# The first gate's row multiplied into the out projection's weights instead of into its result

## The reference

```
sh1, sc1, gt1, sh2, sc2, gt2 = split(silu(c) @ w_ada + b_ada)
h = rms_norm(x) * (1 + sc1) + sh1
proj = h @ w_in                      # split into HGRN2, attention, gates ga, gb
merged = sigmoid(ga) * (y_a @ w_branch_a) + sigmoid(gb) * (y_b @ w_branch_b)
x = x + (1 + gt1) * (merged @ w_out)
h2 = rms_norm(x) * (1 + sc2) + sh2
u_gate, u_val = split(h2 @ w_up)
x = x + (1 + gt2) * ((gelu(conv(u_gate)) * u_val) @ w_down)
return rms_norm(x)
```

## Time and profile before

| what | us |
| --- | --- |
| median of three runs | 940.07 |
| profiled execution, its own time | 939.99 |
| span of the profiled execution | 938.1 |
| TensorE busy with matmuls | 909.8 |
| GpSimd busy | 442.5 |
| VectorE busy | 441.2 |
| ScalarE busy | 363.7 |

### The profile page before, as it was taken

The page is one execution under the profiler, slowest core; times in us unless marked ns, Lnnn a source line. Parts: engine busy times, 40 slices in busy tenths (PEclk is TensorE's granted clock), DMA queues, the critical chain, the costliest instruction groups (busy, mean ns, idle before and its releaser), DMA issues.

```text
span 938.1 us, 11737 instructions
## 1 busy us (share of the span) xinstructions
PE 909.8 (97%) x4468; PEld 768.6 (82%) x4468; DVE 441.2 (47%) x712; ACT 363.7 (39%) x482; POOL 442.5 (47%) x390
## 2 busy tenths in 40 slices
PE   2999999999999999999999999999999999999996
PEld 1888898988878888888888888888888888888885
DVE  4743468684548978976624526222232222200005
ACT  5433335252443323353422237544444444421113
POOL 2589335253424432454554645554444554444554
PEclk9999999999999999999999999999999999999998
DMA  9842221212352858244526221422233222232212
GB/s 312 276 133 90 90 90 45 90 45 91 106 164 90 270 185 264 90 152 168 198 90 224 89 90 46 134 89 89 93 115 105 89 89 89 93 132 90 89 45 90
DMA packets 94087, 115.52 MB, mean 123 GB/s; under 512 B 2206, under 2 KB 84314, under 8 KB 94046
## 3 DMA queue, kind: packets, MB, share of 16 engines
q1 hardware_dynamic: 94046, 114.95, 37.1%
HBM read 112.81 MB, written 2.13 MB: 123 GB/s over the span
## 4 chain that ended last, share of the span: by engine, by line
PE 46%; issue 29%; POOL 20%; DVE 3%; ACT 1%; DMA 1%; POOLq 0%; SPq 0%; DVEq 0%; ACTq 0%
PE bank L1070 45%; POOL w_lo L679 19%; DMA x_in<-in_x_dram 1%; DVE bank L1530 0%; DVE bank L2032 0%; DVE x L2033 0%; PE bank L1073 0%; DVE xn_ffn L1924 0%; POOL masks L616 0%; ACT w_hi L758 0%; POOL masks L653 0%; DVE h_tmp2a L1586 0%; ACT h_tmp L785 0%; POOLq L709 0%; POOL xg L733 0%
## 5 line engine op out<-in xcount | busy, mean ns | idle before, releaser
L679 POOL TENSOR_TENSOR w_lo<-w_raw,w_hi 128x512 fp32r<-128x512 f32 x292 | 390.5, 1368 | 442.4 <-ACT w_hi L758 437.5
L1070 PE MATMUL bank<-h_hi,w_hi 128*128 128x512 f32 (+1 forms) x880 | 340.8, 390 | 0.1
L1070 PE MATMUL bank<-h_lo,w_hi 128*128 128x512 f32 (+1 forms) x880 | 337.2, 386 | 0.0
L1070 PE MATMUL bank<-h_hi,w_lo 128*128 128x512 f32 (+1 forms) x880 | 261.8, 386 | 0.0
L758 ACT ACTIVATE w_hi<-w_raw 128x2048 fp32r<-128x2048 f32 x72 | 137.6, 1911 | 223.4 <-PE bank L1070 223.4
L1070 PEld LDWEIGHTS bank<-h_hi,w_lo 128*128 128x128 f32 x880 | 165.9, 188 | 33.3
L1070 PEld LDWEIGHTS bank<-h_lo,w_hi 128*128 128x128 f32 x880 | 165.9, 188 | 32.9
L1070 PEld LDWEIGHTS bank<-h_hi,w_hi 128*128 128x128 f32 x880 | 165.4, 189 | 33.1 <-POOL h_lo L666 0.3
L1070 PE MATMUL bank<-w_hi,act_hi 128*128 128x512 f32 x176 | 68.5, 389 | 0.0
L1070 PE MATMUL bank<-w_lo,act_hi 128*128 128x512 f32 x176 | 68.5, 389 | 0.0
L1070 PE MATMUL bank<-w_hi,act_lo 128*128 128x512 f32 x176 | 68.5, 389 | 0.0
(11 more groups left out here) (254 smaller groups left out, 1115.2 us busy)
## 6 DMA issues: line engine op xcount, KB each, us to landing
w_raw<-in_w_in_dram SPq DMA_DIRECT2D x32, 1024.0 KB, 5.2
w_raw<-in_w_up_dram SPq DMA_DIRECT2D x22, 1024.0 KB, 5.1
ada<-in_w_ada_dram SPq DMA_DIRECT2D x16, 1024.0 KB, 5.3
w_raw<-in_w_down_dram SPq DMA_DIRECT2D x11, 1024.0 KB, 4.8
ada<-in_w_ada_dram SPq DMA_DIRECT2D x16, 512.0 KB, 8.7
w_raw<-in_w_out_dram SPq DMA_DIRECT2D x4, 1024.0 KB, 5.0
x_in<-in_x_dram SPq DMA_DIRECT2D x4, 512.0 KB, 5.0
w_raw<-in_w_in_dram SPq DMA_DIRECT2D x8, 256.0 KB, 7.4
```

The lines of the kernel that those rows point to most:

```text
L679: ins = pool.tensor_tensor(wlo[slot][:, cols], raw[slot][:, cols], whi[slot][:, cols].bitcast(F32), ALU.subtract)
L1070: return pe.matmul(o, lhsT, rhs, start=start, stop=stop, **kw)
```

## The change

A new function, `gate_out(u)`, multiplies the whole raw unit (128x2048) in place by the matching 512 numbers of the gate's row, repeated for the four blocks of rows, on VectorE. ScalarE's high part of an out unit waits for it by a new semaphore. The multiplication of the result banks is gone, and `added` now waits for the bank itself.

```diff
+        gated_out = sem("gated_out")
...
                     if u == 3:
                         act.wait_ge(hi_done, 3)
+                if U_OUT <= u < U_UP:
+                    act.wait_ge(gated_out, u - U_OUT + 1)
                 high_part(u % 2, 16 * (u // 2 + 1))
...
+            def gate_out(u):
+
+                c = (u - U_OUT) // 2
+                if u == U_OUT:
+                    dve.wait_ge(gate_in[0], 16)
+                dve.wait_ge(raw_in[u % 2], 16 * (u // 2))
+                rows = raw[u % 2][:, :].rearrange("p (k c) -> p k c", c=512)
+                gate = g1_row[:, 512 * c:512 * c + 512].unsqueeze(1).broadcast_to([P, KT // 2, 512])
+                tt(rows, rows, gate, ALU.mult).then_inc(gated_out, 1)
+
             def residual(c, t):
 
-                gated(c, t)
                 added(c, t)
 
-            def gated(c, t):
-
-                b = ready(dve, ("out", c, t))
-                link(tt(b[:, :], b[:, :], g1_row[:, 512 * c:512 * c + 512], ALU.mult))
-
             def added(c, t):
 
-                b, cols = bank[BANKS["out", c, t][0]], slice(512 * c, 512 * c + 512)
+                b, cols = ready(dve, ("out", c, t)), slice(512 * c, 512 * c + 512)
                 release(tt(x1[:, t, cols], x1[:, t, cols], b[:, :], ALU.add), ("out", c, t))
...
                 xn_again(1, slice(0, D))
-                gated(1, 2)
                 make_h2(0, 0)
...
+                if U_OUT <= u < U_UP - 2:
+                    gate_out(u + 2)
                 evacuate(u)
+                if U_OUT - 2 <= u < U_OUT:
+                    gate_out(u + 2)
```

## The result

The changed kernel took 943.39 us (median of 8 runs, 942.71 to 944.09), the kernel before on the same chip 940.19 us (8 runs, 939.28 to 940.49). The ratio is 1.0035, with a 95% interval of 1.0026 to 1.0044: slower by 3.2 us. The forecast was 943.3.

The account below looks back on a forecast made before the run. TensorE, busy 97% of the span, was taken as the bound, already waiting 0.23 us for unit 39's low part. Terms +3.1, +0.5 and -0.3 gave +3.3 on 939.99, hence 943.3 us; 8-in-10 range 941.2 to 945.5.

Parts of the forecast that it names:

- The multiplication costs 2.28: On VectorE, each new 128x2048 multiplication of a raw weight unit by the gate's repeated row takes 2.28 us.
- Unit 38: high part +2.34, TensorE waits 0.7 to 2.3: ScalarE's high part of unit 38 starts 2.34 us later, so TensorE waits 0.7 to 2.3 us for GpSimd's low part.
- Unit 39: +3.1, and +0.5 by collisions: Unit 39 starts 3.1 us later through its multiplication, plus 0.5 from VectorE colliding with GpSimd in unit 37's evacuation.
- +3.7 by the exclusion of VectorE and GpSimd: If unit 40's multiplication held off GpSimd's first instruction of unit 39 by 0.3 or more, the sum became +3.7, not +3.3.
- A wait of 1.2 to 2.9 at unit 39: TensorE finishes unit 38 by 534.7 at most, then waits 1.2 to 2.9 us for unit 39's low part from GpSimd.
- Rival 2: TensorE's pace falls to matmuls 0.43 us apart after a new wait: 945.3, or 947 if at both; chance 0.10.
- matmuls 0.43 apart behind the waits: Sign that the prediction is wrong: TensorE's matmuls after the new waits start 0.43 us apart, against 0.227.
- Units 40 and 41 have cover: Their later weights delay nothing: no TensorE wait at either unit, with 1.4 us of cover at unit 41, plus 0.7 more.
- -0.3 at the second transposition: Tile 3's dropped right-column multiplication shortens TensorE's 0.58 us wait before the second transposition by 0.3, bounds 0 and 0.6.
- The sum: Over the whole kernel, +3.1 for unit 39's multiplication, +0.5 for collisions and -0.3 at the second transposition: +3.3 us.

Follow-up runs that it names:

- early38: The change, with unit 38's multiplication moved ahead of unit 36's evacuation so that only unit 39's chain is late: 945.44 us, ratio 1.0057.
- right_clear: The change for the right columns only (units 40 and 41), whose multiplications also wait until GpSimd finishes the unit before: 944.06 us, ratio 1.0036.
- left: The change for the left columns only (units 38 and 39); right columns multiplied in the result as in the kernel before: 943.85 us, ratio 1.0037.
- final: The change, with unit 38's multiplication ahead of unit 36's evacuation, unit 39's within unit 37's, and ScalarE's high parts of both units earlier: 939.03 us, ratio 0.9993.
- only38: The change, but unit 39's weights are not multiplied and its high part does not wait for the gate: 942.82 us, ratio 1.0027.
- extra1024: The kernel before, plus one unused GpSimd instruction on 1024 columns ahead of unit 38's low part: 943.39 us, ratio 1.0029.

## Why the prediction was right, and where not

The time was right, and the start of unit 39 (536.06, forecast 535.8 to 536.8). By steps:

- *The multiplication costs 2.28.* Three of the four took 2.28 to 2.29 (512.53, and the pair of 4.49 from 526.55, whose records overlap a little), and the fourth 3.10 where GpSimd worked beside it. The repeated row of the gate costs nothing more.
- *Unit 38: high part +2.34, TensorE waits 0.7 to 2.3.* High part at 514.90, +2.19; GpSimd at 516.90, 6.47 long, wait 1.98. Right, at the upper end, as GpSimd lost 1.4 to collisions. The upper bound does not follow from the rows it names: 517.0 and the 5.94 of the earlier trace rows give 522.97 and a wait of 1.6, not 523.7 and 2.3. The 0.7 on top came without a row, and the run used 0.4 of it.
- *Unit 39: +3.1, and +0.5 by collisions.* The high part moved by 3.32 (525.60 to 528.92). The four VectorE instructions that collided lost 0.4, 1.1, 0.4 and 1.1, nearly the series of the prediction, 2.9 in all against 2.6 before. The evacuation ended 0.2 later (526.63; 0.3 by the marks), not 0.5. The mis-sized term is the collisions, by 0.2 to 0.3.
- *+3.7 by the exclusion of VectorE and GpSimd.* The second multiplication of the pair ended at 531.04, 0.13 after GpSimd had started at 530.91, and GpSimd took its undisturbed 5.03. Nothing was lost here.
- *A wait of 1.2 to 2.9 at unit 39.* This is the step that failed in the profiled execution. The prediction said that unit 38 would end by 534.7 and TensorE would wait for the rest. No wait stood there: TensorE worked at half clock in unit 38 and ended it at 536.06. (By their mean clocks, several of the other executions may have kept the pace and waited as forecast.) Rival 2, the fall of the pace, happened, and was given 1 in 10. Its price of 2.0 was near (1.8), but it was added to the sum (945.3), when at the first wait it lies beside the time that unit 39's low part takes anyway. One of the prediction's own marks of error, matmuls 0.43 apart behind the waits, was seen, and it belonged to a cost that was covered. early38 shows the case in which it isn't: +5.0, the bare sum of a late unit 39 and a slow stretch, less the gain at the second transposition. That the time came out within 0.1 of the forecast in spite of this step is owed to the cover, which the prediction had not seen; so in part it is luck.
- *Why I gave it 1 in 10.* The nearest row was a wait of 1.30 with full pace behind it. In these runs the pace was kept behind 0.80, 1.09 and 1.30, and lost behind 1.98, 1.99, 2.35, 2.82 and 3.25. The forecast of 0.7 to 2.3 reached well into the second group, so 1 in 10 was too little. The Trainium skill (TensorE: Matmul & The Clock Gate, section "What's actually happening") names just the two clocks that were seen.
- *Units 40 and 41 have cover.* Yes, no wait there, although unit 40's low part took 7.08. The cover at unit 41 was 1.6 before and not 1.4, because TensorE came at 554.56 and not at 554.4. right_clear shows how small it is: 4.5 us later cost 3.0.
- *-0.3 at the second transposition.* The wait went from 0.58 to 0.21, a gain of 0.37; by the marks the second transposition came 3.13 later where unit 40 had come 3.44 later, a gain of 0.31. left takes the right half out and has 0.6 again.
- *The sum.* By the marks unit 39 starts 3.51 later (3.39 in the times of the profiles, as unit 36 itself started 0.12 earlier), the second transposition 3.13, and the end 3.22; the medians differ by 3.2. What took back the last 0.1 was not looked into.

## What to carry to other kernels

Work taken off an engine with slack gains nothing where TensorE doesn't wait for it (of eight multiplications only the one ahead of the second transposition gave something, 0.3 us), and work put on the weights' chain costs its whole length when TensorE is at the end of that chain: look for the smallest wait of TensorE and ask whose output released it. Two delays one unit apart don't add when the later unit's own chain is as late as the earlier unit has become: here either alone made unit 39 start 3.5 to 3.7 us later, both together 3.5. Mending only the earlier made the kernel slower (943.4 to 945.4). Where the same instruction must be in that chain, place it by what the other engines do at that time: final does the same work as the change and is about 4 us faster. Its two left multiplications stand ahead of the places where they held up the chain, ScalarE's high parts are moved up with them, and the low parts of units 38, 39 and 40 are ready 1.8, 0.9 and 0.4 us before TensorE wants them, collisions included.

## What the runs showed of the hardware

- In all eight profiled executions with a wait of TensorE of 1.98 us or more in the middle of dense work, the granted clock stood at half for about 3.4 us afterwards, and eight or nine matmuls of 128x512 lay 0.43 us apart instead of 0.227. So a wait of 2 us cost nearly 4. It set in at once (after, 1.98) or several matmuls later (only38, 1.99; extra1024, 2.35; early38, 3.25). By the mean clocks of the unprofiled executions it probably doesn't happen every time. Behind waits of 0.80, 1.09 and 1.30 the clock stayed at full. Between 1.30 and 1.98 no run shows it.
- A granted clock of 1.00 in the profile is no proof of full pace near the start of a program: from 24.4 to 28.9 us of the kernel before the windows read 1.00, and the matmuls lie 0.43 apart. The distance of two starts is the safer reading.
- GpSimd's four low parts, 5.03 when VectorE is quiet, took 5.50 to 7.41 beside VectorE's instructions with both inputs in SBUF, and VectorE's 2.29 became 2.35 to 3.37. Short instructions do it too: in extra1024, with no multiplication of weights on VectorE, the evacuation's instructions of 128x512 made the low part of unit 38 take 6.80.
